# Where the expert gates are spread in a two-block transformer kernel: beside the tiles of up and down stages, with down stages in column halves

## The chip, the cores and the metric

The kernel runs on one core of one Trainium2 chip. The metric is device time in microseconds (us), from runs of the whole kernel. TensorE, VectorE, ScalarE, POOL (GpSimd) and SP (which only issues DMAs) each work through an instruction stream of their own; semaphores order them.

## What is computed

Two transformer blocks on 256 tokens of width 2048, all in float32. The first block is a mixer (windowed attention beside a recurrent unit) and then a PEER layer: 8 heads route each token to 16 of 128 x 128 = 16384 experts each. The second block is an SSD mixer and a dilated attention, each with adaLN (shift, scale and gate from a condition vector). The part that the change touches, cut to its core:

```python
def peer(x, w_pq, sub_k1, sub_k2, u_emb, v_emb):
    ...
    sc, sel = lax.top_k(cand, PEER_TOPK)
    eidx = jnp.take_along_axis(cidx, sel, axis=-1)     # i1 * 128 + i2
    gates = jax.nn.softmax(sc, axis=-1)
    ...
        act = jax.nn.gelu(jnp.einsum('cd,ced->ce', xc, u_emb[ic]))
        return jnp.einsum('ce,ced->cd', (gc * act).astype(vc.dtype), v_emb[ic])

def _adaln(c, w, b):
    mod = jax.nn.silu(c) @ w + b
    shift, scale, gate = jnp.split(mod, 3, axis=-1)
```

## The kernel before

**Experts as dense products.** The kernel does not gather experts. It computes gelu(x u) for all 16384, multiplies it by a gate matrix that is zero where an expert was not chosen, and multiplies the result by all of v. Experts are ordered by their second key i2 in 128 chunks of 128 (the first key i1 is the partition), and the chunks in four quarters of `EB` = 32. Each quarter has an up stage (`up0` to `up3`) and a down stage (`down0` to `down3`). The order is up0, down0, up1, down1 and so on; a table (`STREAM`, line 86) gives it and the number of bodies, 16 for each of these stages.

**Tiles.** A body is four weight tiles of 128 x 1024 floats (512 KB). SP loads each into one of four buffers `raw` (line 341). ScalarE rounds it to fp32r, `w_hi` (`high`, line 930); VectorE, or POOL in up0 and xbc, subtracts to get the rest, `w_lo` (`low`, lines 1287 and 402). TensorE multiplies high by high, high by low and low by high. So a tile can be split up to four tiles ahead, and a buffer comes free when TensorE has used it (`tile_used`). In an up stage the tiles are the stationary operand: two tiles make one chunk of 128 experts x 256 tokens in PSUM bank 0 or 1, 48 matmuls of 256 columns (`block_product`, lines 505 to 507). In a down stage (`rows_body`, lines 557 to 561) the chunk of `hid`, staged and split as `st_hi` and `st_lo` (lines 946, 953 and 1305), is stationary and the tile moves, 12 matmuls of 512 columns; all eight PSUM banks hold the sum over a quarter, 256 tokens x 2048. After the stage VectorE adds the eight banks to the residual `X` (`add_product`, line 1477).

**Spreading the gates.** For eight tokens at a time (`n`, 32 of them) VectorE compares the slots' first key to 0..127 (`hot`) and the second to the chunks of the quarter (`hot_one` or `hot_two`, line 1557, `key_rows`); the second is multiplied by the gate, which is held as three bf16 parts: part 0 by VectorE (line 1564), parts 1 and 2 by POOL (line 418). TensorE then makes eight 128 x width matrices, three small matmuls each (`spread`, line 704), 24 in all. ScalarE copies the result out to the *next* quarter's `hid` (`gates_out`, line 1095), and when that quarter's up stage runs, gelu goes to `geluT` (line 1111) and VectorE multiplies it on (line 1609). The first two quarters are made together, width 64, in a stage of their own between up0 and down0, where VectorE also applies the first quarter's gates (`gates_onto_first`, line 1579). The third and fourth quarters' gates are spread in up1 and up2, width 32, two spreads per body; up3 has none.

**Routing's end.** VectorE finds the top 16 of 256 sums and the slots while TensorE runs up0. ScalarE's exp of the chosen scores (line 1084) stands in its queue behind all of up0. VectorE then normalises (lines 1535 to 1537), TensorE transposes the slots (line 691), ScalarE copies them out (lines 1086 to 1088), VectorE splits the gates into parts.

**AdaLN.** The 2048 x 6144 matrices of both layers are read as 384 tiles of 128 x 512 by POOL's DMAs (line 427), and VectorE multiplies each by a column of silu(c) and sums them up in `ada_acc` (line 1572): three per body in down0, up1, down1, up2, down2, up3 and down3, and in z. At the end of each down stage TensorE sums over the partitions, 12 or 24 matmuls of one column (line 733), into PSUM bank 3, after the add of the first half of the tokens.

**The order** is written out by hand, as one instruction stream per engine in program order; a step moved in one stream is moved past all that is queued there.

Of the kernel before, what the change touches and what calls it, by code (L numbers as in the profile page):

```python
# [14 lines left out]
ds = bass.ds  # L15
# [66 lines left out]
for _name, _w in [("d0", DG * P), ("d1", DG * S), ("slopes", DG * DH)]:  # L82
# [14 lines left out]
NB = dict(STREAM)  # L97

# [31 lines left out]
def build(nc, a, out):  # L130
    ctx = ExitStack()
    with ctx:
# [78 lines left out]
        iota_b = sb("iota_b", [P, NK], BF16, peer)  # L211

# [19 lines left out]
        hot1 = sb("hot1", [P, 2, 8, NK], BF16, experts)  # L232
        hot2, hot2_gate = {}, {}
        hot2[EB] = sb("hot2_one", [P, 2, 8, EB], BF16, experts)
        hot2_gate[EB] = sb("hot2_gate_one", [P, 2, 3, 8, EB], BF16, experts)
        ada = sb("ada", [P, 3, ADA], F32, experts)
        two_quarters = ExitStack()
        hot2[2 * EB] = sb("hot2_two", [P, 2, 8, 2 * EB], BF16, two_quarters)
        hot2_gate[2 * EB] = sb("hot2_gate_two", [P, 2, 3, 8, 2 * EB], BF16, two_quarters)
        two_quarters.close()  # L240
        ada_acc = sb("ada_acc", [P, 2, 3, ADA], F32, experts)
        geluT = xtmp
# [10 lines left out]
        gate_diag = sb("gate_diag", [P, 2, D], F32R, spreading)  # L253
        spreading.close()
# [43 lines left out]
        oT = k2T  # L298

# [11 lines left out]
        CHUNKS = {"w_out": 0, "down0": 16, "down1": 48, "down2": 80, "down3": 112, "a_out": 144, "b_out": 176}  # L311
# [10 lines left out]
        def tile_source(name, j, u):  # L322
            if name in ("w_out", "a_out", "b_out"):
                return a[name][2 * j + u // 2][:, (u % 2) * TILE:(u % 2 + 1) * TILE]
            if name[:-1] in ("up", "down"):
                return a[("u" if name[:-1] == "up" else "v") + "_emb"][4 * j + (2 * EB * int(name[-1]) + u)]
            return a[name][4 * j + u]
# [3 lines left out]
        def _(sp):  # L331
# [4 lines left out]
            def weight(name, j, u):  # L336
# [4 lines left out]
                sp.dma_start(raw[:, u, :], tile_source(name, j, u)).then_inc(raw_loaded[u], 16)  # L341

            for name, n in STREAM:
                start = 0
# [15 lines left out]
        def _(pool):  # L360
# [51 lines left out]
            pool.wait_ge(sem("route_over"), 2)  # L412

            def slot_gates(n, n_before, width, r):

                shape = [P, 2, 8, width]
                pool.wait_ge(sem("keys_matched"), n + (n_before + 1))
                pool.tensor_tensor(hot2_gate[width][:, r, 1:3, :, :],  # L418
                                   hot2[width][:, r, :, 0:width].unsqueeze(1).to_broadcast(shape),
                                   slot_gate[:, 1:3, ds(8 * n, 8)].unsqueeze(3).to_broadcast(shape),  # L420
                                   ALU.mult).then_inc(sem("hot2_done"), 1)

            def ada_tiles(seg, k, buffer):

                for q in range(3):
                    pool.wait_ge(sem("ada_used"), 3 * k + (48 * seg + q + 1))
                    pool.dma_start(buffer[:, q, :], a["ada_w"][3 * k + (48 * seg + q)])\  # L427
                        .then_inc(sem(f"ada_loaded{q}"), 16)


            with pool.Fori(0, 16) as j:
                for r in range(2):
                    slot_gates(2 * j + r, 0, 2 * EB, r)
            for quarter in range(QUARTERS):
                if quarter:
                    with pool.Fori(0, 16) as k:
                        ada_tiles(2 * quarter - 1, k, ada)
# [3 lines left out]
                with pool.Fori(0, 16) as k:  # L441
                    ada_tiles(2 * quarter, k, ada)
# [1552 lines left out]
```

## Time and profile before

| | us |
|---|---|
| three runs | 3894.15, 3888.4, 3893.26 |
| median | 3893.26 |
| span of the profiled execution | 3895.9 (its own total is not given apart from the span) |
| TensorE busy in matmuls | 3431.8 (88% of the span) |
| VectorE busy | 2303.0 (59%) |
| ScalarE busy | 1692.7 (43%) |
| POOL busy | 915.5 (23%) |
| mean granted clock of TensorE | 0.926 of full |

The profile's times are from the start of the span. PE is TensorE's matmuls, PEld its weight loads, DVE VectorE, ACT ScalarE; L505 is line 505 of the kernel. A matmul's listed duration overlaps its neighbours', so the pace of matmuls is read from the length of a stretch and their count, not from the mean. PEclk is the granted clock of TensorE, 1.00 being 2.4 GHz and 0.50 being 1.2 GHz. A row of a group ends with the idle time of the engine just before its instructions and who ended most of it.

### The profile page before, as it was taken

Reading aid. Unit: us, or ns where it says so; the run is one execution under the profiler, and the core shown is the slowest. Engines: PE = TensorE matmul, PEld = TensorE weight load, DVE = VectorE, ACT = ScalarE, POOL = GpSimd, SP = SyncE. Lnnn points to the kernel's source line nnn. Section 1 sums busy time; section 2 is a strip of 40 time slices with the busy share of each in tenths; the row PEclk is TensorE's granted clock in tenths of the full one; section 3 lists DMA queues with packets and bytes.
Section 4 is the critical chain, followed back from the end, with each engine's and each line's share of the span. In section 5 each row is a group of like instructions: output and inputs, shape, how many; then the busy total and the mean of one; then the engine's idle time right before and its main releaser. Section 6 shows DMA issues by size and latency. Waiting matters only on the chain.

```text
span 3895.9 us, 69368 instructions
## 1 busy us (share of the span) xinstructions
PE 3431.8 (88%) x23514; PEld 3096.4 (79%) x23514; DVE 2303.0 (59%) x3112; ACT 1692.7 (43%) x2243; POOL 915.5 (23%) x744
## 2 busy tenths in 40 slices
PE   7964899936999999999999997999998897998986
PEld 6953799925889888997799776998777686977975
DVE  4534549197678866896756664334555565444454
ACT  4434446512445543344434443665343344434443
POOL 1300008853123311431111113884111100000000
PEclk9967999956999999999999998999999898999998
DMA  6500444503866686667867772554443354554522
GB/s 199 166 22 32 162 163 156 174 14 97 265 205 209 194 264 213 215 214 236 265 205 250 244 252 72 184 181 154 144 142 121 126 193 141 178 173 146 182 98 87
DMA packets 181787, 656.13 MB, mean 168 GB/s; under 512 B 23040, under 2 KB 23184, under 8 KB 180576
## 3 DMA queue, kind: packets, MB, share of 16 engines
q1 hardware_dynamic: 149328, 545.82, 42.5%
q0 software_dynamic: 32400, 109.56, 9.3%
q8 instruction: 34, 0.56, 0.1%
q14 instruction: 25, 0.20, 0.0%
HBM read 653.18 MB, written 2.10 MB: 168 GB/s over the span
## 4 chain that ended last, share of the span: by engine, by line
PE 76%; DVE 9%; issue 7%; ACT 3%; POOL 3%; DVEq 1%; DMA 1%; ACTq 0%; POOLq 0%; SPq 0%; PEldq 0%
PE PS L505 12%; PE PS L506 12%; PE PS L507 12%; PE PS L557 9%; PE PS L561 9%; PE PS L559 9%; PE PS L540 2%; PE PS L542 2%; PE PS L541 2%; POOL w_lo L402 2%; POOL hot_gate_one L418 1%; PE PS L733 1%; PE PS L704 1%; PE PS L822 1%; PE PS L786 1%
## 5 line engine op out<-in xcount | busy, mean ns | idle before, releaser
L930 ACT ACTIVATE w_hi<-raw 128x1024 fp32r<-128x1024 f32 x1032 | 1093.2, 1060 | 1696.2 <-PE PS L507 944.9
L1287 DVE TENSOR_TENSOR w_lo<-raw,w_hi 128x1024 fp32r<-128x1024 f32 x872 | 1072.9, 1232 | 1006.7 <-ACT w_hi L930 1003.7
L505 PE MATMUL PS<-xt_hi,w_hi 128*128 128x256 f32 x4608 | 1327.5, 288 | 34.5 <-DVEq L1672 8.9
L506 PE MATMUL PS<-xt_lo,w_hi 128*128 128x256 f32 x4608 | 1313.2, 285 | 0.0
L507 PE MATMUL PS<-xt_hi,w_lo 128*128 128x256 f32 x4608 | 1312.3, 285 | 0.0
L505 PEld LDWEIGHTS PS<-xt_hi,w_hi 128*128 128x128 f32 x4608 | 893.8, 194 | 49.5 <-issue 36.1
L506 PEld LDWEIGHTS PS<-xt_lo,w_hi 128*128 128x128 f32 x4608 | 894.3, 194 | 0.0
L507 PEld LDWEIGHTS PS<-xt_hi,w_lo 128*128 128x128 f32 x4608 | 893.8, 194 | 0.0
L557 PE MATMUL PS<-w_hi,st_hi 128*128 128x512 f32 x1472 | 580.4, 394 | 40.5 <-DVE st_lo L1305 40.5
L559 PE MATMUL PS<-w_hi,st_lo 128*128 128x512 f32 x1472 | 578.9, 393 | 0.0
L561 PE MATMUL PS<-w_lo,st_hi 128*128 128x512 f32 x1472 | 578.1, 393 | 0.0
L402 POOL TENSOR_TENSOR w_lo<-raw,w_hi 128x1024 fp32r<-128x1024 f32 x160 | 402.1, 2535 | 241.7 <-ACT w_hi L930 241.7
L427 POOL DMA_DIRECT2D ada<-in_ada_w x336 | 181.7, 541 | 929.0 <-DVE ada_acc L1572 913.3
L557 PEld LDWEIGHTS PS<-w_hi,st_hi 128*128 128x128 f32 x1472 | 280.3, 190 | 100.5 <-issue 42.2
L561 PEld LDWEIGHTS PS<-w_lo,st_hi 128*128 128x128 f32 x1472 | 280.1, 190 | 59.3
L559 PEld LDWEIGHTS PS<-w_hi,st_lo 128*128 128x128 f32 x1472 | 280.4, 190 | 58.6
L1572 DVE SCALAR_TENSOR_TENSOR ada_acc<-ada,silu_c,ada_acc 128x512 f32<-128x512 f32 x336 | 250.2, 745 | 0.0
L418 POOL TENSOR_TENSOR hot_gate_one<-hot_one,slot_gate 128x512 bf16<-128x512 bf16 x64 | 120.7, 1887 | 165.6 <-DVE hot_one L1557 165.1
L540 PE MATMUL PS<-w_hi,xt_hi 128*128 128x512 f32 x352 | 139.4, 396 | 10.0 <-ACT v2n L1245 6.2
L541 PE MATMUL PS<-w_hi,xt_lo 128*128 128x512 f32 x352 | 138.6, 394 | 0.0
L542 PE MATMUL PS<-w_lo,xt_hi 128*128 128x512 f32 x352 | 138.6, 394 | 0.0
L494 POOL COPY q_st<-q2T 128x768 f32 x8 | 6.6, 828 | 538.9 <-PEq L870 499.1
(350 smaller groups left out, 3073.3 us busy)
## 6 DMA issues: line engine op xcount, KB each, us to landing
raw<-in_u_emb SPq DMA_DIRECT2D x256, 512.0 KB, 3.9
raw<-in_v_emb SPq DMA_DIRECT2D x256, 512.0 KB, 4.3
ada<-in_ada_w POOLq DMA_DIRECT2D x336, 256.0 KB, 3.7
raw<-in_xbc SPq DMA_DIRECT2D x96, 512.0 KB, 3.2
raw<-in_z SPq DMA_DIRECT2D x80, 512.0 KB, 3.2
raw<-in_q SPq DMA_DIRECT2D x64, 512.0 KB, 3.2
raw<-in_a_out SPq DMA_DIRECT2D x64, 512.0 KB, 4.2
raw<-in_k SPq DMA_DIRECT2D x48, 512.0 KB, 3.2
```

Of the source, the lines that this page charges most:

```text
L402: pool.tensor_tensor(w_lo[:, u, :], raw[:, u, :], w_hi[:, u, :].bitcast(F32), ALU.subtract)\
L505: pe.matmul(o, w_h, x_h, start=start, stop=False, skip_group_check=True)
L506: pe.matmul(o, w_h, x_l, start=False, stop=False, skip_group_check=True)
L507: return pe.matmul(o, w_l, x_h, start=False, stop=stop, skip_group_check=True)
L540: pe.matmul(o, xt_hi[:, k, t], w_hi[:, u, c:c + 512], start=k == 0, stop=False)
L541: pe.matmul(o, xt_lo[:, k, t], w_hi[:, u, c:c + 512], start=False, stop=False)
L557: pe.matmul(o, st_hi[:, s, t], w_hi[:, u, c], start=first and s == 0, stop=False, skip_group_check=True)
L559: pe.matmul(o, st_lo[:, s, t], w_hi[:, u, c], start=False, stop=False, skip_group_check=True)
L561: last = pe.matmul(o, st_hi[:, s, t], w_lo[:, u, c], start=False, stop=stop and s == 1, skip_group_check=True)
L930: act.activation(w_hi[:, u, :], raw[:, u, :], ACT.Copy).then_inc(hi_done, 1)
L1287: dve.tensor_tensor(w_lo[:, u, :], raw[:, u, :], w_hi[:, u, :].bitcast(F32), ALU.subtract)\
L1572: dve.scalar_tensor_tensor(acc[:, q, :], buffer[:, q, :], silu_c[:, ds(k, 1)], acc[:, q, :], ALU.mult, ALU.add).then_inc(sem("ada_used"), 1)
```

## The change

- **Order.** The stages run up0, up1, down0, up2, down1, up3, down2, down3.
- **Spreads.** The stage of its own is gone, and so are POOL's gate products, `gates_out` and `geluT`. Gelu is written straight to `hid`, without gates. The gates of quarter q are spread in the next up stage (quarters 0, 1 and 2 in up1, up2 and up3) and those of quarter 3 in down2, all with width 32. VectorE multiplies them from PSUM onto `hid` (`apply`). The one-hot matrices are laid out with the eight tokens innermost, so that VectorE's operands are adjacent and TensorE reads both of its operands with a step of eight elements; VectorE makes all three gate parts in one operation.
- **Down stages** run over all chunks for columns 0 to 1023 (banks 0 to 3, `half` 0), and then over all of them again for columns 1024 to 2047 (banks 4 to 7). Each chunk is staged twice, in four slots (`st_hi`, `st2_hi`) in place of two. The add of a half follows its eight bodies (`add_half`). In down2 the spreads use banks 4 and 5, then 2 and 3.
- **Routing.** ScalarE's exp stands after nine bodies of up0, the slots' transposes after thirteen. The table of keys is copied eight times wide (`iota8`).
- **AdaLN.** Tiles per body: two in up1 to up3, three in down0, down1, down3, z, a_out, k2 and the first four bodies of v2, none in down2. The sums over partitions follow in the next stage, behind its first body (or behind all of xbc, z, k2 and two thirds of v2), into bank 7. The memsets of the new accumulators `ada_acc_a` and `ada_acc_k` stand before a_out's first group norm and before k2.

The diff, cut to its core:

```diff
 STREAM = [
-    ("up0", 16), ("down0", 16), ("up1", 16), ("down1", 16),
-    ("up2", 16), ("down2", 16), ("up3", 16), ("down3", 16),
+    ("up0", 16), ("up1", 16), ("down0", 16), ("up2", 16), ("down1", 16),
+    ("up3", 16), ("down2", 16), ("down3", 16),
...
+            if name[:-1] == "down":
+                return a["v_emb"][8 * j + (2 * (EB * int(name[-1]) + u - EB * half) + half)]
...
# the TensorE stream
-            channel_blocks("up0", act_free, ACT_BLOCKS["up0"])
+            with pe.Fori(0, 13) as j:
+                up_body("up0", j)
             pe.wait_ge(sem("slots_done"), 1)
...
             last.then_inc(sem("slots_turned"), 1)
+            with pe.Fori(13, 16) as j:
+                up_body("up0", j)
...
-            def spread(n, n_before, width, r):
+            def spread(n, n_before, r, bank):
                 pe.wait_ge(sem("hot_done"), 2 * n + (2 * n_before + 2))
-                pe.wait_ge(sem("hot2_done"), n + (n_before + 1))
-                pe.wait_ge(sem("gates_out"), n + (n_before + 1))
+                pe.wait_ge(sem("gates_applied"), n + (n_before + 1))
                 for t in range(8):
                     for part in range(3):
-                        last = pe.matmul(PS[:, 4 + r, t * width:(t + 1) * width], hot1[:, r, t, :],
-                                         hot2_gate[width][:, r, part, t, 0:width], start=part == 0, stop=part == 2,
+                        last = pe.matmul(PS[:, bank, t * EB:(t + 1) * EB], hot1[:, r, :, t],
+                                         hot2_gate[:, r, part, :, t], start=part == 0, stop=part == 2,
                                          skip_group_check=True)
...
+            def up_stage(quarter, n_before):
+                if quarter > 1:
+                    pe.wait_ge(sem("peer_added"), 2 * quarter - 3)
+                def spread_body(j):
+                    for b in range(2):
+                        spread(2 * j + b, n_before, b, 2 + b)
+                        pe.wait_ge(act_free, 2 * j + (ACT_BLOCKS[up] + b + 1))
+                        block_product(up, j, b, PS[:, b, 0:S])
+                spread_body(0)
+                if quarter > 1:
+                    pe.wait_ge(sem("peer_added"), 2 * quarter - 2)
+                    ada_sum(f"down{quarter - 2}", 3, acc_down)
+                with pe.Fori(1, 15) as j:
+                    spread_body(j)
+                for b in range(2):
+                    spread(30 + b, n_before, b, 2 + b)
+                up_body(up, 15)
...
+            def down_tile(name, j, u, half, start=False, stop=False, last_block=None):
+                pe.wait_ge(lo_done, 4 * (j + FIRST_BODY[name]) + u + 1)
+                pe.wait_ge(stage_lo_done, 4 * j + (CHUNKS[name] + u + 1))
+                for tt in (1, 0):
+                    if tt == 0 and last_block:
+                        pe.wait_ge(act_free, last_block)
+                    for g in range(2):
+                        o = PS[:, 4 * half + 2 * tt + g, :]
...
+            up_stage(1, 0)
+            down_stage(0, 0, False, True)
+            up_stage(2, EB)
+            down_stage(1, 0, False, True)
+            up_stage(3, 2 * EB)
+            down_stage(2, 3 * EB, True, True)
+            down_stage(3, 0, False, False)
...
# the ScalarE stream
+            bodies("up0", first_gelu, 0, 9)
             act.wait_ge(sem("pick_shifted"), 1)
             act.activation(pick[:, :, :], pick[:, :, :], ACT.Exp).then_inc(sem("pick_exp"), 1)
+            bodies("up0", first_gelu, 9, 4)
             act.wait_ge(sem("slots_turned"), 1)
...
+            bodies("up0", first_gelu, 13, 3)
...
# the VectorE stream
-            def key_rows(n, n_before, base, width, r):
+            def key_rows(n, n_before, base, r):
                 def match(o, first, w, row):
-                    keys = iota_b[:, first:first + w].unsqueeze(1).to_broadcast([P, 8, w])
-                    return dve.tensor_tensor(o, keys, slotsT[:, row, ds(8 * n, 8)].unsqueeze(2).to_broadcast([P, 8, w]),
+                    return dve.tensor_tensor(o, iota8[:, first:first + w, :],
+                                             slotsT[:, row, ds(8 * n, 8)].unsqueeze(1).to_broadcast([P, w, 8]),
                                              ALU.is_equal)
...
+            def apply(n, n_before, quarter, bank):
+                dve.wait_ge(sem("gates_spread"), n + (n_before + 3))
+                x = hid[quarter % 2][:, :, ds(8 * n, 8)]
+                dve.tensor_tensor(x, x, PS[:, bank, 0:8 * EB].rearrange("p (t b) -> p b t", t=8), ALU.mult)\
+                    .then_inc(sem("gates_applied"), 1)
...
+                def body(j):
+                    for u in range(4):
+                        low(j + (f + 1), u)
+                        if u % 2 == 0:
+                            key_rows(2 * j + (2 + u // 2), n_before, (quarter - 1) * EB, u // 2)
+                            apply(2 * j + u // 2, n_before, quarter - 1, 2 + u // 2)
+                        else:
+                            ada_product(f"up{quarter}", j, u // 2, ada, acc_up)
...
+            def add_half(quarter, half):
+                dve.wait_ge(tile_used, 4 * (FIRST_BODY[f"down{quarter}"] + 8 * half + 8))
...
+                for tt in (1, 0):
+                    x = X[:, tt, half * TILE:half * TILE + TILE]
+                    last = dve.tensor_tensor(x, x, banks(4 * half + 2 * tt, 2), ALU.add)
+                last.then_inc(sem("peer_added"), 1)
...
+                def body(j, first_chunk, half):
+                    for u in range(4):
+                        low(j + (f + 1), u)
+                        stage_hid(quarter, first_chunk + u, 4 * j + (4 + u), u)
+                        if spreading and u in ((0, 1) if half == 0 else (1, 3)):
+                            b = u if half == 0 else u // 2
+                            key_rows(2 * j + (2 + b), n_before, 3 * EB, b)
+                            apply(2 * j + b, n_before, 3, 4 - 2 * half + b)
+                        if products and u:
+                            ada_product(f"down{quarter}", j, u - 1, ada, acc_down)
```

## Rows read from the trace of the kernel before

**Rows 1.** The page of the profile, part 4: the chain that ended last, by engine
```profile
PE 76%; DVE 9%; issue 7%; ACT 3%; POOL 3%; DVEq 1%; DMA 1%; ACTq 0%; POOLq 0%; SPq 0%; PEldq 0%
```
**Rows 2.** View by stretches: length, busy PE, PEld, DVE, ACT, POOL; PEclk, DMA share, GB/s
```profile
779.30:791.70 12.40, 1.66 (x8) 1.14 (x6) 6.42 (x10) 4.09 (x7) 5.46 (x3) 0.67 0.30 108
...
791.70:931.80 140.10, 46.07 (x769) 41.85 (x769) 137.78 (x128) 12.98 (x34) 84.11 (x34) 0.50 0.02 6
...
1108.50:1119.30 10.80, 5.47 (x26) 5.35 (x26) 6.77 (x5) 2.34 (x2) 1.07 (x2) 0.63 0.51 185
...
1119.30:1343.10 223.80, 213.47 (x2304) 208.49 (x2304) 195.57 (x238) 126.46 (x158) 84.72 (x78) 0.99 0.62 198
...
1343.10:1348.40 5.30, 0.17 (x8) 0.10 (x4) 5.00 (x8) 1.40 (x5) 1.07 (x2) 0.84 0.82 230
...
1348.40:1525.00 176.60, 176.60 (x768) 145.79 (x768) 118.06 (x141) 76.00 (x93) 24.68 (x46) 0.99 0.79 254
...
1525.00:1541.00 16.00, 10.68 (x50) 10.50 (x50) 6.82 (x5) 1.06 (x1) 1.07 (x2) 0.58 0.35 125
...
1957.00:2143.10 186.10, 186.10 (x1536) 185.99 (x1535) 120.06 (x144) 75.09 (x94) 24.67 (x46) 0.99 0.76 238
...
2324.60:2345.90 21.30, 10.63 (x50) 10.34 (x49) 11.96 (x11) 6.64 (x7) 0.54 (x1) 0.62 0.29 103
```
**Rows 3.** The groups of instructions in the stretch 791.7 to 931.8
```profile
L1564 DVE TENSOR_TENSOR hot_gate_two<-hot_two,slot_gate 128x512 bf16<-128x512 bf16 x31 | 73.7, 2378 | 0.0
...
L704 PE MATMUL PS<-hot_gate_two,hot 128*128 128x64 bf16 x768 | 46.1, 240 | 97.0 <-DVE hid L1579 88.1 <-DVE hot_gate_two L1564 8.8
```
**Rows 4.** TensorE's timeline (start, length): two spreads, in different stages
```profile
927.05 1.44 PE L704 MATMUL PS<-hot_gate_two,hot 128*128 128x64 bf16 x24 [2.94 <-DVE hid L1579]
...
1148.58 0.77 PE L704 MATMUL PS<-hot_gate_one,hot 128*128 128x32 bf16 x24
```
**Rows 5.** The groups of instructions of the whole run, shapes apart
```profile
L930 ACT ACTIVATE w_hi<-raw 128x1024 fp32r<-128x1024 f32 x1032 | 1093.2, 1060 | 1696.2 <-PE PS L507 944.9 <-PE PS L561 587.3 <-PE PS L542 154.4
...
L1287 DVE TENSOR_TENSOR w_lo<-raw,w_hi 128x1024 fp32r<-128x1024 f32 x872 | 1072.9, 1232 | 1006.7 <-ACT w_hi L930 1003.7 <-DVE convT L1402 2.5
...
L1572 DVE SCALAR_TENSOR_TENSOR ada_acc<-ada,silu_c,ada_acc 128x512 f32<-128x512 f32 x336 | 250.2, 745 | 0.0
...
L1557 DVE TENSOR_TENSOR hot<-iota_b,slotsT 128x1024 bf16<-128x1024 bf16 x96 | 116.7, 1215 | 0.0
...
L704 PE MATMUL PS<-hot_gate_one,hot 128*128 128x32 bf16 x1536 | 48.8, 177 | 16.3 <-POOL hot_gate_one L418 12.6 <-DVE hot_gate_one L1564 3.8
...
L1305 DVE TENSOR_TENSOR st_lo<-hid,st_hi 128x256 fp32r<-128x256 f32 x128 | 53.2, 418 | 0.1
...
L1557 DVE TENSOR_TENSOR hot_one<-iota_b,slotsT 128x256 bf16<-128x256 bf16 x64 | 26.7, 417 | 0.7 <-DVE ada_acc L1597 0.7
...
L1579 DVE TENSOR_TENSOR hid<-hid,PS 128x256 f32 x30 | 12.2, 408 | 0.0
...
L1613 DVE MEMSET ada_acc<- 128x1536 f32 x4 | 5.4, 1338 | 1.2 <-ACT st_hi L953 0.8 <-DVE hid L1579 0.4
```
**Rows 6.** Timeline of VectorE and TensorE at the routing's end
```profile
693.92 4.42 DVE L1533 TENSOR_REDUCE slots<-pqT 128x256 f32<-128x4096 f32 x1
...
782.67 0.42 DVE L1535 TENSOR_REDUCE rsum<-pick 128x16 f32<-128x256 f32 x1 [84.33 <-ACT pick L1084]
...
783.90 1.54 PE L691 MATMUL PS<-cc,slots 128*128 128x128 f32 x6 [4.48 <-DVE slots L1537]
```
**Rows 7.** Timeline of VectorE, TensorE and ScalarE behind the last down stage
```profile
2327.79 4.48 DVE L1477 TENSOR_TENSOR X<-X,PS 128x2048 f32<-128x2048 f32 x2
...
2330.13 10.40 PE L733 MATMUL PS<-cc,ada_acc 128*128 128x1 f32 x48 [5.33 <-DVE X L1477]
...
2337.65 0.29 ACT L971 ACTIVATE stat<-stat,pc 128x2 f32<-128x2 f32 x1
...
2341.21 4.62 DVE L1646 SCALAR_TENSOR_TENSOR X<-X,stat,row 128x2048 f32<-128x2048 f32 x2
```

More of the change, by code:

```diff
@@ L97 @@
 NB = dict(STREAM)
+ADA_STAGES = [("up1", 2), ("down0", 3), ("up2", 2), ("down1", 3), ("up3", 2), ("down3", 3),
+              ("z", 3), ("a_out", 3), ("kv2", 3)]
+ADA_SEGMENT = {"down0": 2, "down1": 4, "down3": 6, "z": 7, "a_out": 1, "kv2": 3}
+ADA_LOADS = {}
+for _slot in range(3):
+    _n = 0
+    for _name, _w in ADA_STAGES:
+        if _slot < _w:
+            ADA_LOADS[_name, _slot] = _n
+            _n += 16
 class Chain:
@@ L309, in build @@
         DVE_BLOCKS = {"rec": 0, "xbc": 8}
-        CHUNKS = {"w_out": 0, "down0": 16, "down1": 48, "down2": 80, "down3": 112, "a_out": 144, "b_out": 176}
+        CHUNKS = {"w_out": 0, "down0": 16, "down1": 80, "down2": 144, "down3": 208, "a_out": 272, "b_out": 304}
         z_bank = (7, 2)
@@ new lines, in ada_sum @@
+            def ada_sum(stage, count, acc):
+                for q in range(count):
+                    pe.wait_ge(sem(f"ada_used{q}"), ADA_LOADS[stage, q] + 17)
+                for q in range(count):
+                    for c in range(4):
+                        last = pe.matmul(PS[:, 7, 4 * q + c:4 * q + c + 1], acc[:, q, c * P:c * P + P],
+                                         ones[:, 0:1], start=True, stop=True, skip_group_check=True)
+                last.then_inc(sem("ada_summed"), 1)
@@ new lines, in down_stage, with body @@
+            def down_stage(quarter, more=False):
+                f = FIRST_BODY[f"down{quarter}"]
+                def body(j, first_chunk):
+                    for u in range(4):
+                        high(j + (f + 1), u)
+                        stage_hid(quarter, first_chunk + u, u)
+                with act.Fori(0, 7) as j:
+                    body(j, 4 * j + 4)
+                body(7, 0)
+                with act.Fori(8, 15) as j:
+                    body(j, 4 * j - 28)
+                for u in range(4):
+                    high(f + 16, u)
+                    if more and u == 0:
+                        act.wait_ge(sem("gates_applied"), 2 + EB * (quarter + 2))
+                    if more:
+                        stage_hid(quarter + 1, u, u)
@@ L1120, in _ @@
+            up_stage(1)
+            down_stage(0)
+            up_stage(2)
+            down_stage(1)
+            up_stage(3)
+            down_stage(2, more=True)
+            down_stage(3)
+            act.wait_ge(sem("peer_added"), 2 * QUARTERS)
             for tt in range(TT):
@@ new lines, in _ @@
+            for r in range(2):
+                key_rows(r, 0, 0, r)
+            dve.wait_ge(act_free, 2 + ACT_BLOCKS["up0"] + EB)
+            dve.wait_ge(lo_done, 4 * (FIRST_BODY["up1"] + 1))
+            up_stage(1, 0)
+            down_stage(0, sums=True, next_spread=(EB, EB))
+            up_stage(2, EB)
+            down_stage(1, sums=True, next_spread=(2 * EB, 2 * EB))
+            up_stage(3, 2 * EB, next_spread=(3 * EB, 3 * EB))
+            dve.wait_ge(act_free, 2 + ACT_BLOCKS["up3"] + EB)
@@ L1642, in _ @@
+            down_stage(2, 3 * EB, spreading=True, sums=True, products=False, more=True)
+            down_stage(3)
             dve.wait_ge(sem("rms_root"), 4)
```

445 lines of the change are left out of this document (259 added, 186 removed).

## The prediction

> **What bounds the kernel now.** I read the chain of waits first. In the page's part on the chain TensorE's matmuls hold 76% of the span [rows 1], so only two things move the end: matmul time, and stretches where TensorE stands. I then cut the run at TensorE's own gaps, from the last matmul of the first up stage (779.3 us) to the transposes behind the peer block (2345.9 us). That is 1566.6 us, all the change touches but for small sums. [Rows 2] shows three kinds of stretch. In 791.7:931.8 the matmuls are busy 46.07 of 140.1 us at granted clock 0.50: this is the spreading of the gates with nothing beside it. In stage windows TensorE is busy throughout: a down stage takes 176.6 us, an up stage without spreads (the fourth) 186.1 us. Between them lie handoffs: 10.8 and 16.0 us from down to up, 5.3 us from up to down, and 21.3 us at the end. A second down-to-up handoff of 16.0 (1941.0:1957.0) and two more up-to-down ones (5.2 and 5.7) repeat the pattern.
>
> Why is the lone stage slow? A spread's 24 matmuls take 1.44 us there [rows 4], but 140.1 / 32 = 4.4 us pass per spread. VectorE sets it: its first gate product costs 2.38 us each [rows 3], on top of two matches. In the second up stage the same 24 matmuls take 0.77 us [rows 4], at full clock and half the width, and they cost less than VectorE's work, which hides behind tiles. Before these 64 spreads TensorE stands 16.3 us in all, 12.6 of it for POOL's gate product [rows 5].
>
> **The change, part by part.** All terms are against the profiled execution, whose span is 3895.9 us. The runs' median, 3893.26, is 2.6 us under it; that execution's own total is not shown, so I take 2.6 off at the end.
>
> *Lone stage gone.* 140.1 us go, and most of the 12.4 before it [rows 2]. The routing's arithmetic ended at 693.92 + 4.42 = 698.3, then VectorE waited 84.33 us for an exp queued on ScalarE behind the whole up stage [rows 6]. Now that exp stands after nine bodies (16 bodies end at 779.3, each 186.1 / 16 = 11.6 us, so near 698) and TensorE's six transposes after thirteen, near 745. They take 1.54 us [rows 6]. Behind them ScalarE does the gate copy, a key copy eight times wider and the slot copy. The wide key copy has no row; a 128x1024 copy takes 1.06 us [rows 5], and I take 1.1, with 0.3 and 2.2 as ends. It is hidden: tiles are split ahead by up to four buffers, 2.9 us each. Two more table loads on ScalarE hide there too. Left on TensorE: 1.4 us.
>
> *Spreads beside tiles.* Before: 64 beside tiles, 32 wide ones alone. After: 4 x 32 = 128, all 32 columns wide, in up1, up2, up3 and down2. Their price is the sum's largest unknown. The matmul count is the same, but both operands are now read with a step of eight elements (16 bytes), where before they were adjacent. No row has such a read on TensorE. From below: as adjacent, 0.77 us (0.032 us a pair). From above, for this case: 1.44, the lone stage's spread at half clock [rows 4], as if everything took twice the time. VectorE's gate application reads PSUM 128 bytes apart in 408 ns against 418 ns for a same-sized split of neighbours [rows 5], which speaks for the low end on that engine, not for TensorE, which loads a weight tile every 0.03 us. Neither end is nearer in kind, so I take the middle, 1.10 us: 128 x 1.10 = 140.8 us.
>
> *Stages.* Without the cold start that each handoff brings (mean clock 0.99 in the up window, 0.98 to 0.99 in the down one [rows 2]: 1% of 186.1, 1.5% of 176.6) three up stages take 3 x 184.2 = 552.6 and four down stages 4 x 174.0 = 696.0. Column halves change neither the number of tiles nor the matmuls per tile, nor SP's issues (same count, size, order of buffers).
>
> *What stages cost the others.* Each hidden chunk is now split twice: 32 more operations per down stage on ScalarE and VectorE, 0.42 us each [rows 5]. An up body (four tiles) then asks of VectorE, even with no operation getting faster: 4 x 1.23 for the low parts, 2 x (0.42 + 1.22) for matches, 2 x 0.92 for the wider gate product (768 elements at the pace of 1024 in 1.22), 2 x 0.41 for application, 2 x 0.74 for adaLN: 12.4 us against TensorE's 11.5 + 2 x 1.10 = 13.7. In down2: 4 x (1.23 + 0.42) + 2 x 2.97 = 12.5 against 10.9 + 2.2 = 13.1. So VectorE stays below. The old body took 223.8 / 16 = 14.0 with VectorE busy 195.57 us [rows 2]. POOL loses its gate products, so the 12.6 us of waits for them go, and keeps only adaLN's DMAs (two or three per body, as or fewer than before).
>
> *Handoffs.* With halves in banks 0 to 3 and 4 to 7, the residual add of one half (two pieces, together half of 4.48 us [rows 7]) runs under the other half's tiles or the next stage's first body. VectorE's queue then holds the next low part back by about 2 us of four tiles' cover (11 us). The memset of 1.34 [rows 5] and the first splits move under tiles too. I leave 0.5 us for each of seven boundaries, 3.5 in all. One wait is new: in down2 the spreads of the second half use banks of the first, so the second tile waits for the half's add: high part 1.06, low part 1.23, split 0.42, add 2.24, with hops some 5.4 us, minus a tile of 176.6 / 64 = 2.76: 2.7 us. What queues behind it on TensorE is only that tile.
>
> *AdaLN sums.* 48 of the 1-column matmuls now stand inside the stages; 48 took 10.40 us at half clock [rows 7], 0.22 each. At full clock between 0.11 and 0.22: 5.3 to 10.4, I take 7. Their accumulators are ready a body earlier.
>
> *The end.* The 10.40 us of sums leave it. But ScalarE's squares and root end at 2337.9 behind both adds, and VectorE's scaling starts at 2341.2 [rows 7]. The last add is half as long, so the squares end 2.2 sooner, and the scaling starts 3.3 + 2.2 - 0.2 = 5.3 sooner (0.2 for the reciprocal): 21.3 becomes 16.0.
>
> *Later stages.* A memset (1.34) now stands before the first group norm on the path; 36 sum matmuls follow xbc, k2 and part of v2, some under evacuations. I take 5 in all, with 2 and 10 as ends. In a_out, k2 and v2 VectorE gains 3 x 0.74 per body of 11 us, and POOL issues three DMAs; both have room. The second norm's row DMA stands behind POOL's adaLN loads, which end a stage earlier than it is needed.
>
> **Sum.** 552.6 + 696.0 + 140.8 + 7 + 3.5 + 2.7 + 1.4 + 16.0 = 1420.0 us in place of 1566.6: 146.6 less; with the 5 later, 141.6 less. Span 3754.3, time **3752 us**. With the spread at 0.77 it is 3710, at 1.44 it is 3795.
>
> **Rivals.**
> *A, the step costs double.* Every pair of a spread takes twice the adjacent time: 2 x 0.77 = 1.54 us, 128 x 0.44 = 56 us more than my sum: 3808. For it: it is TensorE's only new access pattern, where it loads fastest. Against: VectorE shows no price for distance. The Trainium skill, page "SBUF — State Buffer", section "Specifications (TRN2)", speaks for it: lines are 16 bytes and want two hits each for full rate, and a step of 16 bytes has one. By that rule the time would be this rival's; no row here shows it.
> *B, slower than before.* The stepped weights lose the fast load altogether and pass at the pace of the 4-byte tiles, 186.1 / 1536 = 0.121 us [rows 2]. A spread is then 24 x 0.121 = 2.9 us, 128 x 1.80 = 230 us more than my sum: 3982. It turns the sign from 2.2 us per spread on (1.10 + 141.6 / 128). The 32 spreads of up1 would show it at once. Against: they are still 2-byte operands, 128 wide.
> *C, VectorE becomes the bound*, the lock step of low parts, matches and application making every spreading stage as long as the old up1: 3 x (223.8 - 219.4) + (223.8 - 209.2) = 28 us more: 3780. For: bodies fill 90 to 95% of VectorE at old durations. The Trainium skill, page "VectorE: DVE Perf Modes", section "What auto-detection actually checks", says that 16-bit operands with step 1 run two elements a cycle; the old match (1024 in 1.22 us) repeats its slot along the inner axis, the new one does not. By that, the match would be half as long and C gone.
> *D, handoffs don't overlap*, the change not doing what it says: a wait I overlooked (an add, a staged chunk) keeps each of seven at 5.3: 7 x 4.8 = 34 us more: 3786.
>
> **Chances.** Forecast (spreads between 0.77 and 1.4) 0.50, A 0.20, B 0.10, C 0.06, D 0.08, the rest mixed. The range takes in the cheap spread with cheap sums (3700) and A with a little lost beside (3815), and leaves out B. A difference of 0.2% (8 us) is about what a measurement of this kernel can tell from none; all cases but B lie past it on the fast side. Faster 0.87, same 0.02, slower 0.11.
>
> **What will show it.** Right: no stretch at clock 0.5 between the first up stage and the end of down3; three up stages alike, near 219 us, down0, down1 and down3 near 175, down2 near 210; no TensorE idle above 1 us at a boundary; VectorE busy under 95% in up1. The length of 24 spread matmuls (0.77 to 1.4, 1.5 or 2.9) decides between the forecast, A and B. Wrong: an idle before each spread whose releaser is VectorE (C), or one at the boundaries released by an add or a split (D), or ScalarE standing for the slots inside up0 while TensorE runs out of tiles.

## The result and the profile after

The changed kernel takes **3827.06 us** (median of 4 runs, 3824.03 to 3831.45) against 3893.7 for the kernel before beside it: a ratio of 0.983, 95% interval 0.9815 to 0.9843. It is faster by 1.7%, where 3.6% was forecast (3752 us), and it lies 12 us above the range. The profiled execution took 3831.45 us, its span 3829.8.

Parts 1 and 4 of the page of the changed kernel (busy time by engine; the chain that ended last, by engine and by line) answer to [rows 1]:

```profile
PE 3511.7 (92%) x24282; PEld 3180.7 (83%) x24282; DVE 2229.5 (58%) x3351; ACT 1650.6 (43%) x2237; POOL 711.1 (19%) x648
...
PE 83%; DVE 5%; issue 3%; ACT 3%; POOL 2%; PEld 2%; DMA 1%; DVEq 0%; ACTq 0%; SPq 0%; POOLq 0%; PEldq 0%
```

TensorE's share of the chain rose from 76 to 83%, and VectorE's fell from 9 to 5%, as it should with the lone stage and the handoffs gone. The view by stretches, with the columns of [rows 2], has one row per stage: up1, down0, up2, down1, up3, down2 up to its last spread, the rest of it with down3, and the end:

```profile
784.00:1020.60 236.60, 236.59 (x2304) 235.31 (x2305) 152.02 (x225) 76.38 (x98) 19.78 (x34) 0.99 0.58 177
1020.60:1197.00 176.40, 176.31 (x787) 145.76 (x785) 134.21 (x179) 86.49 (x125) 25.86 (x49) 1.00 0.83 261
1197.00:1436.20 239.20, 239.20 (x2329) 237.92 (x2329) 154.80 (x232) 77.49 (x99) 16.92 (x32) 0.99 0.57 176
1436.20:1612.60 176.40, 176.31 (x787) 145.78 (x785) 134.20 (x179) 86.45 (x125) 26.01 (x49) 1.00 0.83 261
1612.60:1854.30 241.70, 240.89 (x2329) 239.39 (x2328) 155.89 (x236) 78.15 (x100) 17.16 (x32) 0.99 0.57 175
1854.30:2078.00 223.70, 218.32 (x1483) 183.02 (x1484) 145.67 (x249) 82.60 (x122) 1.07 (x2) 0.98 0.48 148
2078.00:2266.00 188.00, 188.00 (x840) 155.57 (x839) 140.16 (x185) 90.64 (x131) 24.15 (x45) 0.99 0.78 248
2266.00:2282.20 16.20, 0.28 (x3) 0.05 (x1) 9.52 (x8) 6.64 (x7) 0.53 (x1) 0.64 0.42 142
```

In all but down2 and the end TensorE is busy from edge to edge, so most of the missing time is inside its busy time. A down stage is as forecast, 176.4 us with sums and boundary. An up stage is not: 236.6 to 241.7 where near 219 was forecast. The stretch 1566.6 us long before, and forecast at 1420.0, is 1500.0 now (782.1, the first up stage's last matmul, to 2282.15). The groups of instructions of the whole run, shapes apart, say which of its work grew:

```profile
L732 PE MATMUL PS<-hot_gate,hot 128*128 128x32 bf16 x3072 | 216.9, 242 | 7.8 <-DVE hid L1720 3.0 <-DVE hot_gate L1712 2.5 <-DVE X L1787 2.4
L732 PEld LDWEIGHTS PS<-hot_gate,hot 128*128 128x128 bf16 x3072 | 199.8, 163 | 20.4 <-issue 8.9 <-DVE hot_gate L1712 4.9 <-DVE X L1787 2.8
```

The spread's matmuls hold TensorE 216.9 us for 128 spreads, 1.69 us each, where the same shape took 48.8 us for 64, 0.76 each [rows 5]. The last matmul's end lies under the tile that follows, so a busy time says too much of the path. TensorE's timeline has a spread and the start of the tile behind it, here first in the changed kernel and then in the one with adjacent operands (the first experiment):

```profile
792.85 1.72 PE L732 MATMUL PS<-hot_gate,hot 128*128 128x32 bf16 x24
794.38 0.36 PE L525 MATMUL PS<-xt_hi,w_hi 128*128 128x256 f32 x1
```

```profile
799.98 0.77 PE L734 MATMUL PS<-hot_gate,hot 128*128 128x32 bf16 x24
800.59 0.36 PE L527 MATMUL PS<-xt_hi,w_hi 128*128 128x256 f32 x1
```

From start to start it is 1.53 us against 0.61. The expectations below reckon with such times, the groups with busy times. What a spread adds to the path, with the slower first matmuls of the tile behind it, comes from the up stages: (236.6 - 184.2 - 1.7) / 32 = 1.58 (1.7 for a start at a low clock, below), so about 1.6 against the 1.10 taken.

### The profile page after: what moved, and what is told of

The parts are those of the page before. It is cut to its first block, busy times and chain, and to the rows that moved or that the text cites. A ratio compares the mean times of both kernels' runs of the same rounds, so it can differ in the third digit from the quotient of the medians.

```text
span 3829.8 us, 70643 instructions
## 1 busy us (share of the span) xinstructions
PE 3511.7 (92%) x24282; PEld 3180.7 (83%) x24282; DVE 2229.5 (58%) x3351; ACT 1650.6 (43%) x2237; POOL 711.1 (19%) x648
## 4 chain that ended last, share of the span: by engine, by line
PE 83%; DVE 5%; issue 3%; ACT 3%; POOL 2%; PEld 2%; DMA 1%; DVEq 0%; ACTq 0%; SPq 0%; POOLq 0%; PEldq 0%
PE PS L525 13%; PE PS L526 13%; PE PS L527 13%; PE PS L779 6%; PE PS L781 6%; PE PS L783 6%; PE PS L732 5%; PE PS L577 3%; PE PS L579 3%; PE PS L581 3%; PE PS L560 2%; PE PS L561 2%; PE PS L562 2%; POOL w_lo L426 2%; PE PS L933 1%
## 5 line engine op out<-in xcount | busy, mean ns | idle before, releaser
L440 POOL DMA_DIRECT2D ada<-in_ada_w x240 | 128.8, 537 | 1345.0 <-DVE acc_down L1728 680.9
L779 PEld LDWEIGHTS PS<-w_hi,st_hi 128*128 128x128 f32 x1024 | 194.2, 190 | 40.4 <-ACT hid L1218 1.0
L783 PEld LDWEIGHTS PS<-w_lo,st_hi 128*128 128x128 f32 x1024 | 193.3, 189 | 40.6
L781 PEld LDWEIGHTS PS<-w_hi,st_lo 128*128 128x128 f32 x1024 | 193.6, 189 | 39.3
L732 PE MATMUL PS<-hot_gate,hot 128*128 128x32 bf16 x3072 | 216.9, 242 | 7.8 <-DVE hid L1720 3.0
L732 PEld LDWEIGHTS PS<-hot_gate,hot 128*128 128x128 bf16 x3072 | 199.8, 163 | 20.4 <-issue 8.9
```

The lines of the kernel that those rows point to most:

```text
L732: last = pe.matmul(PS[:, bank, t * EB:(t + 1) * EB], hot1[:, r, :, t], hot2_gate[:, r, part, :, t], start=part == 0, stop=part == 2, skip_ ...
L779: pe.matmul(o, st(st_hi, st2_hi, u)[:, t], w_hi[:, u, c], start=start, stop=False, skip_group_check=True)
L781: pe.matmul(o, st(st_lo, st2_lo, u)[:, t], w_hi[:, u, c], start=False, stop=False, skip_group_check=True)
L783: last = pe.matmul(o, st(st_hi, st2_hi, u)[:, t], w_lo[:, u, c], start=False, stop=stop, skip_group_check=True)
```

## The experiments

Each kernel was timed beside the kernel before, which stood between 3891 and 3897 us each time. All but the last three keep the change's order of work and alter only in which order the one-hots of eight tokens lie in SBUF: K tokens innermost, so that TensorE reads them with a step of 2 K bytes (the change has K = 8).

**All adjacent (K = 1 for both operands).**

```
-        hot1 = sb("hot1", [P, 2, NK, 8], BF16, experts)
-        hot2_gate = sb("hot2_gate", [P, 2, 3, EB, 8], BF16, experts)
+        hot1 = sb("hot1", [P, 2, 8 // K1, NK, K1], BF16, experts)
+        hot2_gate = sb("hot2_gate", [P, 2, 3, 8 // K2, EB, K2], BF16, experts)
...
-    pe.matmul(..., hot1[:, r, :, t], hot2_gate[:, r, part, :, t], ...)
+    pe.matmul(..., hot1[:, r, t // K1, :, t % K1], hot2_gate[:, r, part, t // K2, :, t % K2], ...)
```

> The changed kernel with the one-hot matrices back in the old layout (tokens outermost, keys adjacent), nothing else. Theory W: what the forecast missed is the price of TensorE's stepped reads, so 24 spread matmuls go from 1.55 us back to 0.62 and 128 x 0.93 = 119 us fall away: 3708, or up to 3730 if VectorE, whose matches go back from 0.68 to 1.22 us, fills its bodies (12.4 us asked against 12.9 of TensorE). Rival X: spreads beside tiles are dear for another reason (the switch between 4-byte and 2-byte tiles): they stay near 1.5 us, time 3827 or above.

Measured: 3722.49 us (3720.78 to 3724.96), ratio to before 0.956 (0.9545 to 0.9577), 104.6 us less than the changed kernel. Its groups of instructions, TensorE's spread and VectorE's two matches and gate product (the last three in the stretch 784 to 2180):

```profile
L734 PE MATMUL PS<-hot_gate,hot 128*128 128x32 bf16 x3072 | 98.0, 177 | 19.0 <-DVE hid L1739 10.0 <-DVE hot_gate L1725 6.8 <-DVE X L1806 2.1
...
L1710 DVE TENSOR_TENSOR hot<-iota,slotsT 128x1024 bf16<-128x1024 bf16 x127 | 154.8, 1219 | 0.0
L1725 DVE TENSOR_TENSOR hot_gate<-hot,slot_gate 128x768 bf16<-128x768 bf16 x128 | 124.0, 968 | 0.0
L1710 DVE TENSOR_TENSOR hot<-iota,slotsT 128x256 bf16<-128x256 bf16 x127 | 53.2, 419 | 0.0
```

The spread is back at 98.0 / 128 = 0.77 us, and with it went 119 us of matmul time. VectorE is slower here (its match 1219 ns, in the changed kernel 684) and still TensorE waited for it only 18.9 us in all. So the step of the reads cost the time, not the switch between tiles and small matmuls, and VectorE, at the old durations, was not the bound.

**Two tokens innermost (K = 2, a step of 4 bytes).** The same edit; the gate product becomes three operations, one a part.

> Both one-hot layouts keep 2 tokens innermost, so the spread's weight loads and matmul operands step by 4 bytes in place of 16; everything else is the changed kernel's, but that the gate product is three operations. Theory W1 (only a wide step costs: the price comes with the 16-byte step): spread near 0.65 to 0.80 us, time 3715 to 3740, as with adjacent elements (3722). Theory W2 (any step costs, adjacent or not is what counts): spread still 1.4 to 1.6 us, time 3815 to 3835. In between (price grows with the step, about a half left): spread near 1.0 us, 3755 to 3790.

Measured: 3712.0 us (3709.82 to 3712.97). The spread costs as little as when adjacent, so a step of 4 bytes costs nothing, and VectorE keeps its short match, since its innermost axis still runs over tokens (its two lines in the stretch 784 to 2180):

```profile
L734 PE MATMUL PS<-hot_gate,hot 128*128 128x32 bf16 x3072 | 98.1, 177 | 13.5 <-DVE hid L1739 6.3 <-DVE hot_gate L1730 4.9 <-DVE X L1806 2.4
L1730 DVE TENSOR_TENSOR hot_gate<-hot,slot_gate 128x256 bf16<-128x256 bf16 x381 | 87.4, 284 | 0.0
L1710 DVE TENSOR_TENSOR hot<-iota,slotsT 128x1024 bf16<-128x1024 bf16 x127 | 86.9, 684 | 0.0
```

**Four tokens innermost (K = 4, 8 bytes).**

> Both layouts keep 4 tokens innermost: the spread's operands step by 8 bytes. With 4 bytes the spread was as short as adjacent (3712 us), with 16 bytes 1.51 us (3827 us). Theory W1a (a threshold between 8 and 16 bytes): spread near 0.61 to 0.80 us, time 3705 to 3725. Theory W1b (the price grows with the step, from 8 bytes on): spread 1.0 to 1.3 us, 3760 to 3795. W1c (8 bytes cost as much as 16): 1.5 us, 3810 to 3830.

Measured: 3737.47 us (3735.27 to 3740.17), between the first two expectations:

```profile
L734 PE MATMUL PS<-hot_gate,hot 128*128 128x32 bf16 x3072 | 124.6, 191 | 12.7 <-DVE hid L1739 5.5 <-DVE hot_gate L1730 4.9 <-DVE X L1806 2.4
```

124.6 / 128 = 0.97 us a spread. Eight bytes cost a quarter more, sixteen bytes 2.2 times as much: a price that starts between 4 and 8 bytes.

**Which operand pays? Only the stationary one stepped (K = 8 and 1), then only the moving one (1 and 8).**

> Only the one-hot that the spread's first operand (the stationary one, loaded as weights) reads keeps the 16-byte step; the gate product, the moving one, has adjacent elements. If the weight load pays (128 columns of 32 rows each against 32 moving columns): spread 1.4 to 1.6 us, time 3820 to 3840, as VectorE keeps the slow form of the gate product too. If the moving side pays: spread 0.61 to 0.7 us, 3715 to 3730. If both pay their part: near 1.0 us, 3765 to 3785.

> The reverse: the stationary one-hot has adjacent elements, and the gate product (the moving operand, 32 columns) keeps the 16-byte step. If the weight load pays: spread 0.61 to 0.7 us, time 3715 to 3730. If the moving side pays: 1.4 to 1.6 us, 3815 to 3835. If both pay their part: near 1.0 us, 3760 to 3780.

Measured: 3827.32 us (3826.63 to 3827.88) and 3815.8 us (3810.42 to 3821.03). The spread's group in the first and in the second:

```profile
L734 PE MATMUL PS<-hot_gate,hot 128*128 128x32 bf16 x3072 | 208.4, 213 | 10.3 <-DVE hid L1739 4.4 <-DVE hot_gate L1725 3.6 <-DVE X L1806 2.3
L734 PEld LDWEIGHTS PS<-hot_gate,hot 128*128 128x128 bf16 x3072 | 196.8, 170 | 23.0 <-issue 10.5 <-DVE hot_gate L1725 6.0 <-DVE X L1806 2.8
```

```profile
L734 PE MATMUL PS<-hot_gate,hot 128*128 128x32 bf16 x3072 | 204.6, 238 | 10.4 <-DVE hid L1739 4.6 <-DVE hot_gate L1721 3.5 <-DVE X L1806 2.3
L734 PEld LDWEIGHTS PS<-hot_gate,hot 128*128 128x128 bf16 x3072 | 182.6, 116 | 23.8 <-issue 9.8 <-DVE hot_gate L1721 7.5 <-DVE X L1806 2.7
```

Each run came out as if its side alone paid, which the expectations took to exclude each other. Either side alone costs nearly all of it, 1.63 and 1.60 us a spread, and both together 1.69: the prices are not added, and the sum of halves (3760 to 3785 us) is not seen. This fits a load of the next weights that runs beside the matmul, with the slower of the two setting the pace (208.4 and 196.8 us are busy side by side); no run separates the two. To mend only one side, the weights alone, would have gained 11 us of 105.

**A step of 32 bytes on the moving side.** `hot2_gate` gets rows of 16 tokens of which 8 are used.

> As the kernel in which only the moving operand steps (16 bytes, 3816 us, 1.41 us a spread), but its rows are 16 tokens wide of which 8 are used, so that the step is 32 bytes. Theory (the price comes once each element stands in a 16-byte line of its own, and more distance costs nothing): spread 1.35 to 1.45 us, 3812 to 3820. Rival (the price grows with the step, as from 4 to 8 to 16 bytes): spread 2.0 us or more, 3885 or later.

Measured: 3817.25 us (3815.31 to 3819.45), with the spread as before:

```profile
L734 PE MATMUL PS<-hot_gate,hot 128*128 128x32 bf16 x3072 | 205.0, 238 | 10.4 <-DVE hid L1739 4.5 <-DVE hot_gate L1721 3.5 <-DVE X L1806 2.3
```

205.0 against 204.6 us: from 16 to 32 bytes, on the moving side, distance costs nothing more.

**The routing's end behind the whole first up stage again.**

```
-            with pe.Fori(0, 13) as j:
+            with pe.Fori(0, 16) as j:
                 up_body("up0", j)
...
-            with pe.Fori(13, 16) as j:
-                up_body("up0", j)
...
-            bodies("up0", first_gelu, 0, 9)
+            bodies("up0", first_gelu, 0, 16)
             act.wait_ge(sem("pick_shifted"), 1)
...
-            bodies("up0", first_gelu, 9, 4)
...
-            bodies("up0", first_gelu, 13, 3)
```

> The changed kernel with one part of the change undone: ScalarE's exp, TensorE's six transposes and the copies behind them stand behind all sixteen bodies of the first up stage again, and not behind the ninth and the thirteenth. Theory (the routing's end was on the path and its move is worth what stood between the last matmul of the first up stage and the first spread, 12.4 us and the waits of the first key rows): 3839 to 3847, with 14 to 20 us between the first up stage's last matmul and the first spread, where the changed kernel has 1.9. Rival (it was covered by something else, such as the split tiles): within 4 us of 3827.

Measured: 3831.62 us (3828.65 to 3836.99), 4.6 more than the changed kernel: too little for the theory and just past the rival's edge. The start of the profiled executions varies by some us, so the trace is read between two marks: from the first matmul that scores the keys to the first spread. It is 784.55 - 565.48 = 219.1 us here and 784.01 - 572.37 = 211.6 in the changed kernel: 7.4 us. TensorE's transposes start 4.5 us after the up stage, released by the slots:

```profile
779.30 1.54 PE L718 MATMUL PS<-cc,slots 128*128 128x128 f32 x6 [4.48 <-DVE slots L1681]
```

The same stretch was 791.7 - 570.08 = 221.6 us in the kernel before, so the two kernels differ there by 10.0 us, near the forecast (12.4 off, 1.4 on: 11.0). With the exp back in its place 7.4 of these 10.0 us came back. The other 2.5 did not, at least in part because the first spread waits for a gate product of 0.55 us where it was 2.38 [rows 3]. The expectation had 14 to 20 us between the first up stage's last matmul (774.54) and the first spread (784.55), and 10.0 pass: it added the wait for the first key rows to the 12.4, which already held it.

**The handoffs put back.** TensorE waits for the residual add of what it just finished, in the middle and at the end of each down stage:

```
-                    pe.wait_ge(sem("peer_added"), 2 * quarter - 3)
+                    pe.wait_ge(sem("peer_added"), 2 * quarter - 2)
...
                 if quarter:
-                    pe.wait_ge(sem("peer_added"), 2 * quarter - 1)
+                    pe.wait_ge(sem("peer_added"), 2 * quarter)
...
-                if quarter:
-                    pe.wait_ge(sem("peer_added"), 2 * quarter)
+                pe.wait_ge(sem("peer_added"), 2 * quarter + 1)
                 if sums:
```

> The changed kernel, but at each boundary TensorE waits for the residual add of what it just finished: before an up stage and before the last down stage for both halves of the down stage ahead, and in each down stage's middle for its first half's add. That is six more waits than the changed kernel has. Theory (the column halves hide the adds, and each would cost a split in progress, 1.2 us, the two adds of 1.21 us and the hops, 4 to 5.5 us): six gaps of 4 to 5.5 us and 24 to 33 us more, 3851 to 3860. Rival (VectorE reaches the adds in any case later or earlier than that, since its queue is full of splits and adaLN products): gaps of 8 us or more and over 3870, or under 2 us and under 3840.

Measured: 3881.89 us (3874.09 to 3887.78), 54.8 us more than the changed kernel and nearly the kernel before (ratio 0.9965, 0.9952 to 0.9977). That is the rival's time, over 3870, but not its gaps of 8 us. TensorE's waits in the stretch 784 to 2290 (what it waited for: us, times, longest):

```profile
PE PS L779 <- DVE X L1786: 27.3, 5, 5.7
PE PS L732 <- DVE X L1786: 12.2, 2, 6.1
```

Seven waits, 39.5 us, of which the changed kernel has one of 2.4. From matmul to matmul the gaps are 5.5 to 6.5 us, 42.2 in all, 39.5 more than in the changed kernel. The other 15 us are in the view by stretches (columns as above), first a gap, then the twelve us behind it in thirds:

```profile
1199.80:1206.30 6.50, 0.40 (x3) 0.04 (x1) 6.41 (x9) 1.06 (x1) 0.55 (x1) 0.82 0.85 256
1206.30:1210.30 4.00, 4.00 (x36) 4.00 (x37) 0.91 (x1) 0.00 (x0) 0.00 (x0) 0.50 0.07 27
1210.30:1214.30 4.00, 4.00 (x33) 4.00 (x33) 0.95 (x1) 1.06 (x1) 0.00 (x0) 0.93 0.00 0
1214.30:1218.30 4.00, 4.00 (x46) 3.96 (x45) 3.77 (x7) 1.34 (x2) 0.00 (x0) 1.00 0.48 135
```

Behind the gap TensorE is granted its lower level, 1.2 GHz (0.50), for 4 us, and 0.93 in the 4 us after: 4 x 0.50 + 4 x 0.07 = 2.3 us of work not done. Seven times that is 16, about the 15 us. It is an estimate from one gap: the clock fell behind each of the seven, but at other places too, and not at the same ones as in the changed kernel. A handoff's price is its gap and what the clock costs behind it, near 8 us (54.8 / 7), and both theories had priced the gap alone.

**Two-byte pairs and three waits taken away.** To K = 2 come three changes of order: TensorE releases the first key rows ahead of the last three bodies of the first up stage; in down2 the second half's first spreads stand one tile later; and its last two, which stood back to back, stand before different tiles.

```
             last.then_inc(sem("slots_turned"), 1)
+            pe.sem_inc(sem("gates_spread"), 2)
             with pe.Fori(13, 16) as j:
                 up_body("up0", j)
             pe.wait_ge(sem("route_over"), 2)
-            pe.sem_inc(sem("gates_spread"), 2)
...
-                        if spreading and u in ((0, 1) if half == 0 else (1, 3)):
-                            b = u if half == 0 else u // 2
+                        if spreading and u in ((0, 1) if half == 0 else (2, 3)):
+                            b = u if half == 0 else u - 2
...
-                if spreading:
-                    for b in range(2):
-                        spread(30 + b, n_before, b, 2 + b)
                 for u in range(4):
+                    if spreading and u < 2:
+                        spread(30 + u, n_before, u, 2 + u)
                     down_tile(down, 15, u, 1, stop=u == 3)
```

> The layout with 2 tokens innermost (3712 us), and three waits taken away by order alone: TensorE releases the first two key rows ahead of the last three bodies of the first up stage (the gap there is 4.2 us), the first two spreads of the third quarter's down stage's second half stand one tile later (gap 2.7), and its last two spreads stand before different tiles (gap 4.2). Theory (each gap is a wait that a tile's time covers): all three gaps under 1 us, 8 to 11 us less, 3701 to 3705. Rival (the work behind them on VectorE is late as a whole, and the gap only moves to a later tile): 3709 to 3714.

Measured: **3697.37 us** (3694.05 to 3699.13), ratio to before 0.9496 (0.9483 to 0.9509): 14.6 us under K = 2 alone and 129.7 under the changed kernel, the best version here. TensorE's waits over the peer block, first in the kernel with K = 2, then in this one:

```profile
PE PS L734 <- DVE hid L1739: 6.3, 4, 4.0
PE PS L734 <- DVE hot_gate L1730: 4.9, 2, 3.9
PE PS L734 <- DVE X L1806: 2.4, 1, 2.4
```

```profile
PE PS L734 <- DVE hid L1738: 3.5, 4, 1.2
PE PS L734 <- DVE hot_gate L1729: 1.0, 1, 1.0
```

Two gaps are gone (4.2 us each) and the third fell from 2.7 to 1.6, not under 1 as expected. From the key scores to the end of the peer block the trace is 11.4 us shorter (1594.3 to 1583.0), some 9 us of it the gaps. The rest of the difference lies 2.4 us ahead of that stretch and 1.8 behind it, where the two kernels are the same and executions vary.

## Why the prediction was wrong, point by point

**The step that failed is one term: "so I take the middle, 1.10 us: 128 x 1.10 = 140.8 us".** The spread adds 1.6 us to the path: 128 x 0.5 = 64 us of the 75.5 by which the span was missed (3829.8 against 3754.3). With adjacent operands, and VectorE slower for it, the changed kernel takes 3722 us. The true value lay not between the ends but past the upper one, 1.44. That end was the lone stage's spread, an old layout at half clock: it told what a slow clock costs and nothing of a stepped read, so it bounded nothing. That VectorE pays no price for distance was given weight, though the text itself said that it spoke for another engine. (The row behind it, line 1579 of the kernel before, reads PSUM 256 bytes apart and not 128.)

**Rival A was the mechanism**, with 0.20: the step makes every pair dearer. That its 1.54 us meets the measured 1.6 is in part luck. It doubled 0.77, a duration that runs on under the next tile; from start to start the adjacent spread takes 0.61, and the stepped one, 1.53, is 2.5 times that. Its time, 3808, lacks the terms below.

The Trainium skill's rule that stood beside it (page "SBUF — State Buffer", section "Specifications (TRN2)": 16-byte lines, two hits each for full rate) gave the right sign at 16 bytes, and the runs agree that 32 bytes cost no more. It states no factor; the double was the prediction's, and the busy time grew 2.2 times. At 8 bytes a line has two hits, and by the rule the rate would be full; measured is 0.97 us against 0.77, so there it promises too much.

**The rest of the miss.** The stretch is 80 us over its forecast: 64 by the spreads; 3 by the sums, 96 records of 0.106 us = 10.2 where 7 was taken; some 12 at the lower clock level, which the sum put at nothing; 1.9 us ahead of the first spread; and 4.4 us of waits in down2 of which nothing was said, one of 1.1 us at its start and one of 3.2 before its last spread. To the good are the transposes' 1.4 us, which now lie ahead of the stretch, and most of the 3.5 allowed for boundaries (down0 has 0.7 us over its 174.0 and its sums). All this makes 81.

The 1.9 us ahead of the first spread are a wait for VectorE's gate product. It took 2.74 us there, beside low parts on POOL, where the next one took 0.55; no run tells why:

```profile
781.21 2.74 DVE L1712 TENSOR_TENSOR hot_gate<-hot,slot_gate 128x768 bf16<-128x768 bf16 x1
```

In down2, spreads 30 and 31 stand back to back, and VectorE, which makes the key rows of the second and applies the bank that it overwrites, has a low part and a split to do first; it had itself stood 2.48 us for ScalarE's high part, which waits for a buffer. The timeline of VectorE and TensorE (start, length), other tiles left out:

```profile
2073.19 1.68 PE L732 MATMUL PS<-hot_gate,hot 128*128 128x32 bf16 x24
...
2074.53 1.23 DVE L1435 TENSOR_TENSOR w_lo<-raw,w_hi 128x1024 fp32r<-128x1024 f32 x1 [2.48 <-ACT w_hi L1043]
2075.68 0.42 DVE L1777 TENSOR_TENSOR st_lo<-hid,st_hi 128x256 fp32r<-128x256 f32 x1
2076.01 0.89 DVE L1704 TENSOR_TENSOR hot<-iota,slotsT 128x256 bf16<-128x256 bf16 x2
2076.82 0.55 DVE L1712 TENSOR_TENSOR hot_gate<-hot,slot_gate 128x768 bf16<-128x768 bf16 x1
2077.28 0.41 DVE L1720 TENSOR_TENSOR hid<-hid,PS 128x256 f32 x1
2077.85 0.86 PE L732 MATMUL PS<-hot_gate,hot 128*128 128x32 bf16 x11 [2.98 <-DVE hid L1720]
```

The view by stretches for the time at the lower clock level: the start of up1 (two rows), behind up2's first body (up3's is the same, at 1632.3), near up3's end, in down2's first body, and behind two waits in down2:

```profile
784.00:788.00 4.00, 3.99 (x36) 4.00 (x37) 3.84 (x4) 0.00 (x0) 3.27 (x3) 0.73 0.61 163
788.00:792.00 4.00, 4.00 (x30) 4.00 (x30) 1.23 (x2) 1.06 (x1) 0.00 (x0) 0.85 0.58 232
1215.90:1219.30 3.40, 3.40 (x19) 3.40 (x18) 0.00 (x0) 0.00 (x0) 0.54 (x1) 0.50 0.68 214
1840.50:1843.90 3.40, 3.40 (x18) 3.40 (x18) 0.06 (x1) 0.00 (x0) 0.54 (x1) 0.51 0.71 205
1871.60:1874.70 3.10, 3.10 (x10) 2.44 (x9) 0.00 (x0) 0.00 (x0) 0.00 (x0) 0.50 0.63 177
1976.90:1980.50 3.60, 3.60 (x14) 2.83 (x12) 0.00 (x0) 0.00 (x0) 0.00 (x0) 0.53 0.48 147
2079.20:2083.00 3.80, 3.80 (x14) 3.03 (x13) 0.00 (x0) 0.00 (x0) 0.00 (x0) 0.51 0.00 0
```

They are worth 1.1 + 0.6 + 1.7 + 1.7 (up3) + 1.7 + 1.6 + 1.7 + 1.9 us. The prediction's sign of being right, no stretch at clock 0.5 before the end of down3, did not hold. Beside the 80: the first up stage ended 2.8 us later than in the profile of before (2.3 of it already at the first key score, 572.37 against 570.08), and everything behind the peer block took 1547.65 us for 1550.0, where 5 more had been allowed, 7.4 to the good. 80.0 + 2.8 - 7.4 = 75.4.

**What held.** The gains themselves: no lone stage, no handoff over 1.2 us but in down2's middle. Stages: 174.0 a down stage was right to the us. Rival D did not come; with the handoffs put back 55 us were lost, so its price of 34 was too little. The new wait in down2, forecast at 2.7, is 2.7 from matmul to matmul and 2.4 of idle: the next spread starts at 1975.45, released by the half's add. The end, forecast 16.0, is 16.2. POOL's waits are gone.

**Rivals B and C.** B's 2.9 us per spread did not come; its rows of 4-byte tiles were a wrong yardstick too. C did not come: VectorE is busy 152.0 of 236.6 us in up1, and even at its old durations (all adjacent) it set nothing but some waits. The matches took 684 ns for 1215 and 301 for 417 [rows 5], with the slot no longer repeated along the inner axis; where the operands were adjacent for TensorE, the slot was repeated and the match took 1219 ns.

This agrees with the Trainium skill, page "VectorE: DVE Perf Modes", section "What auto-detection actually checks", by which two elements pass a cycle if every tensor is 16-bit with step 1.

## What to carry to other kernels

A layout has two readers: what makes one engine's operation twice as fast (tokens innermost, 0.53 us saved a match on VectorE, which was off the path) made the other's 2.2 times as long (2.5 times from start to start), on the path. An inner block of 4 bytes served both here. When no row shows a new access pattern, a middle between two rows of other things is not an estimate; the case with a mechanism deserves the weight, or the range must reach past it.

Price a wait on TensorE with the clock behind it (here 6 us of gap cost 8), price a duration from the start of one instruction to the start of the next, and look for two uses of a double buffer with no tile between them.

## What the hardware showed that was not expected

A spread's pace, by the step of each operand in bytes (busy time of its group over 128, from the rows above):

| stationary | moving | us a spread | time, us |
|---|---|---|---|
| 2 | 2 | 0.77 | 3722 |
| 4 | 4 | 0.77 | 3712 |
| 8 | 8 | 0.97 | 3737 |
| 2 | 16 | 1.60 | 3816 |
| 2 | 32 | 1.60 | 3817 |
| 16 | 2 | 1.63 | 3827 |
| 16 | 16 | 1.69 | 3827 |

It was not expected that 32 stepped columns of the moving operand cost as much as 128 of the stationary one, nor that the two together cost no more than the slower. Why the two are so alike stays open; other counts of columns were not tried.

The clock fell four times in the changed kernel where TensorE had not stood: at 1215.9, 1632.3, 1840.5 and 1871.6 us. Right ahead of each it had done only small matmuls, 40 or 48 in 2.9 to 4.1 us: the one-column sums and then a spread, or two spreads together.

```profile
1211.71 2.74 PE L743 MATMUL PS<-cc,acc_down 128*128 128x1 f32 x24
1837.32 3.10 PE L732 MATMUL PS<-hot_gate,hot 128*128 128x32 bf16 x48
1868.42 1.84 PE L743 MATMUL PS<-cc,acc_up 128*128 128x1 f32 x16
```

Behind the same two spreads in up1 (1006.2) and up2 (1421.6) it did not fall. So a crowd of small matmuls may cost clock as a gap does; no run was made to show it.
